# Banded attention unrolled into 19 rounds, with its bias table stored during the projection

## The reference, cut to what matters

```
s = einsum('bcqhgd,bckhd->bchgqk', qc, kb) * (HEAD_DIM ** -0.5)
bucket = t5_bucket(kpos[:, None, :] - qpos[:, :, None])
bias = rel_bias[bucket]
s = where(kmask, s + bias[None], -inf)
p = softmax(concatenate([s, sink], axis=-1), axis=-1)[..., :-1]
o = einsum('bchgqk,bckhd->bcqhgd', p, vb)
```

## Time and profile before

| | us |
|---|---|
| median of 3 runs | 2666.45 (2666.01 to 2674.58) |
| profiled execution | 2664.8 |
| its span | 2663.1 |
| TensorE busy in it | 2303.4 (86%) |
| DVE busy | 1716.6 (64%) |
| ACT busy | 1580.6 (59%) |
| POOL busy | 342.8 (13%) |

### The profile page before, as it was taken

The page is one execution under the profiler, slowest core; times in us unless marked ns, Lnnn a source line. Parts: engine busy times, 40 slices in busy tenths (PEclk is TensorE's granted clock), DMA queues, the critical chain, the costliest instruction groups (busy, mean ns, idle before and its releaser), DMA issues. The chain is left out here.

```text
span 2663.1 us, 36661 instructions
## 1 busy us (share of the span) xinstructions
PE 2303.4 (86%) x11322; PEld 1828.2 (69%) x11322; DVE 1716.6 (64%) x3034; ACT 1580.6 (59%) x2365; POOL 342.8 (13%) x425
## 2 busy tenths in 40 slices
PE   5999999917776999999997999279999999999980
PEld 4888888713444777777775888268888888888860
DVE  4314232135544787888774333579999999999986
ACT  5314342134543888877774433157888888788866
POOL 1101111100001000000000000021222222222221
PEclk9989999957886999999998999589999999999995
DMA  6425453151214222222004433279798878998847
GB/s 218 139 83 165 163 175 118 64 108 54 67 47 124 64 62 64 64 64 64 7 9 141 149 135 128 80 288 371 251 302 261 254 235 292 361 321 261 287 111 271
DMA packets 207042, 427.79 MB, mean 161 GB/s; under 512 B 37992, under 2 KB 84408, under 8 KB 205784
## 3 DMA queue, kind: packets, MB, share of 16 engines
q1 hardware_dynamic: 174872, 323.45, 35.6%
q0 software_dynamic: 32080, 103.20, 13.8%
HBM read 445.05 MB, written 86.39 MB: 200 GB/s over the span
## 5 line engine op out<-in xcount | busy, mean ns | idle before, releaser
L2285 DVE TENSOR_TENSOR moe_w_lo<-fetch_w_raw,moe_w_hi 128x1024 fp32r<-128x1024 f32 x376 | 434.9, 1216 | 8.5 <-ACT moe_w_hi L2214 8.3
L2214 ACT ACTIVATE moe_w_hi<-fetch_w_raw 128x1024 fp32r<-128x1024 f32 x376 | 368.3, 1053 | 67.5 <-PEq L90 36.3
L2339 PE MATMUL moe_ps_gu<-moe_w_hi,moe_xT_hi 128*128 128x512 f32 x736 | 293.1, 398 | 4.3 <-DVE moe_xT_lo L2296 4.3
L2341 PE MATMUL moe_ps_gu<-moe_w_hi,moe_xT_lo 128*128 128x512 f32 x736 | 289.0, 393 | 0.0
L2340 PE MATMUL moe_ps_gu<-moe_w_lo,moe_xT_hi 128*128 128x512 f32 x736 | 288.4, 392 | 0.0
L1260 ACT ACTIVATE fox_p<-fox_ps_t,fox_ncumT 128x512 f32<-128x512 f32 (+4 forms) x352 | 209.6, 595 | 117.7 <-PE fox_ps_t L1434 60.5
L461 PE MATMUL proj_ps_chunk<-proj_hT_hi,proj_w_hi 128*128 128x512 f32 (+1 forms) x576 | 234.6, 407 | 4.7 <-DVE proj_hT_lo L400 2.4
L1344 DVE TENSOR_TENSOR fox_p_lo<-fox_p,fox_p_hi 128x512 fp32r<-128x512 f32 (+4 forms) x352 | 199.2, 571 | 55.1 <-ACT fox_p_hi L1261 54.5
L463 PE MATMUL proj_ps_chunk<-proj_hT_hi,proj_w_lo 128*128 128x512 f32 (+1 forms) x576 | 231.4, 402 | 0.0
L462 PE MATMUL proj_ps_chunk<-proj_hT_lo,proj_w_hi 128*128 128x512 f32 (+1 forms) x576 | 230.9, 401 | 0.0
L1324 DVE CUSTOM_DVE_ANT_0 fox_ps_r<-fox_ps_r,fox_ncum 128x512 f32<-128x512 f32 (+4 forms) x352 | 198.0, 592 | 46.9 <-PE fox_ps_r L1404 25.9
(11 more groups left out here) (318 smaller groups left out, 5138.7 us busy)
## 6 DMA issues: line engine op xcount, KB each, us to landing
fetch_w_raw<-in_w_e_gate_dram SPq DMA_DIRECT2D x192, 512.0 KB
fetch_w_raw<-in_w_e_up_dram SPq DMA_DIRECT2D x192, 512.0 KB
fetch_d_raw<-in_w_e_down_dram SPq DMA_DIRECT2D x92, 1024.0 KB
proj_w_raw<-in_w_in_dram SPq DMA_DIRECT2D x24, 1536.0 KB, 8.0
proj_xt<-in_x_dram SPq DMA_DIRECT2D x16, 512.0 KB
h<-proj_hrow POOLq DMA_DIRECT2D x16, 512.0 KB, 3.2
qT<-proj_qk_out POOLq DMA_DIRECT2D x32, 256.0 KB, 3.3
win_q_raw<-qT SPq DMA_DIRECT2D x32, 256.0 KB, 3.8
```

Source lines behind the costliest of these rows:

```text
L2214: nc.scalar.activation(w_hi[:, k], w_raw[:, k].rearrange("p j n -> p (j n)"), ACT.Copy).then_inc(gu_high, 1)
L2285: nc.vector.tensor_tensor(w_lo[:, k], w_raw[:, k].rearrange("p j n -> p (j n)"), w_hi[:, k].bitcast(F32), ALU.subtract).then_inc(gu_split, 1)
L2339: nc.tensor.matmul(out, xT_hi[:, slot, k], w_hi[:, k, cols], start=k == 0, stop=False)
L2341: done = nc.tensor.matmul(out, xT_lo[:, slot, k], w_hi[:, k, cols], start=False, stop=k == KT - 1)
```

## The change

The bias table is now written and stored at the end of superblock 0 of the projection: SP loads `relT` near the projection's start, DVE makes the 31 copies behind the meta tokens' two, and POOL issues the store there. In the attention the three loads of the bias go out from POOL at once, without a wait for a store, and `bias0` is masked first; tile 0 needs only that one.

The hardware loop is gone. Every engine's list is 19 rounds written out. In round n TensorE and DVE make scores and biased scores of tile n, ACT the exponentials of tile n-1, TensorE, DVE and ACT turn and multiply tile n-2, and TensorE and DVE turn back and divide tile n-3. There are four buffers of raw queries and of values, three of split queries and of scores, two of `pT`; the score banks go from four to three, and the banks of turned probabilities from two to three. SP loads queries and values four tiles ahead. Keys are loaded in two pieces and split in four quads of four tiles, the first ahead of round 0, the others in rounds 0 to 2. The steps of the forget gates are spread over rounds 2 to 7. There is one `ntop` operation per tile in place of two, and the small memsets (`tick`, L824) are gone.

```diff
+        relT = m.sb("relT", [A_HEADS, N_BUCKETS])
+        table = m.sb("table", [A_HEADS, BIAS_TAB])
...
+                    pool.wait_ge(table_done, 1)
+                    pool.dma_start(t["table"][:, :, 0:BIAS_TAB],
+                                   table[:].unsqueeze(1).to_broadcast([A_HEADS, P, BIAS_TAB])).then_inc(table_stored, 16)
...
+                    dve.wait_ge(table_in, 16)
+                    for a, b, bucket in bucket_runs(-BIAS_R0, BIAS_TAB - 1 - BIAS_R0):
+                        done = nc.vector.tensor_copy(table[:, a + BIAS_R0:b + BIAS_R0 + 1],
+                                                     relT[:, bucket:bucket + 1].to_broadcast([A_HEADS, b - a + 1]))
+                    done.then_inc(table_done, 1)
...
-        q_raw = m.sb("q_raw", [P, 2, A_HEADS, P])
+        q_raw = m.sb("q_raw", [P, 4, A_HEADS, P])
...
-        s = m.sb("s", [P, 2, A_HEADS, SPAN])
+        s = m.sb("s", [P, 3, A_HEADS, SPAN])
...
-        pT = m.sb("pT", [P, 4, 4 * P])
+        pT = m.sb("pT", [P, 2, 4, 4 * P])
...
-        ps_s = [m.ps(f"ps_s{i}", [P, 2, 256]) for i in range(4)]
-        ps_pT = m.ps("ps_pT", [P, 2, 4 * P])
+        ps_s = [m.ps(f"ps_s{i}", [P, 2, 256]) for i in range(S_BANKS)]
+        ps_pT = [m.ps(f"ps_pT{i}", [P, 4 * P]) for i in range(T_BANKS)]
...
-        def tiles(engine, body):
-            body(0, 0, 0)
-            body(1, 1, 0)
-            body(2, 0, 1)
-            with engine.Fori(1, TILES // 2 - 1) as pair:
-                body(2 * pair + 1, 1, pair)
-                body(2 * pair + 2, 0, pair + 1)
-            body(TILES - 1, 1, TILES // 2 - 1)
...
+        LAST = TILES + 3
+        def rounds(body):
+            for n in range(LAST):
+                body(n)
...
-            sp.wait_ge(table_stored, 16)
...
+            def load_keys(piece, a, b):
+                for kv in range(A_KV):
+                    for half in range(2):
+                        sp.dma_start(k_raw[half * HD:half * HD + HD, kv, a:b],
+                                     t["kT"][kv * HD:kv * HD + HD, a - PAD:b - PAD]).then_inc(k_in[piece], 16)
...
+            load_keys(0, PAD, FIRST)
+            load_queries(0)
+            load_queries(1)
+            load_keys(1, FIRST, PAD + TOK)
+            load_queries(2)
+            load_queries(3)
+            for n in range(4):
+                load_values(n)
...
+            for n in range(4, TILES):
+                load_queries(n)
+                load_values(n)
...
+            for tensor, col, width, rel in ((bias, META, SPAN - META, META - PREV), (bias0, 0, META, -META),
+                                            (bias0, PREV, P, 0)):
+                pool.dma_start(tensor[:, :, col:col + width],
+                               bass.AP(tab.tensor, tab.offset + BIAS_R0 + rel,
+                                       [[BIAS_TAB, P], [P * (BIAS_TAB + 1), A_HEADS], [1, width]])).then_inc(bias_in, 16)
...
+            for n in range(TILES):
+                if n == 8:
+                    pool.wait_ge(dstep, 4)
+                    pool.dma_start(t["ncum"], fa[:]).then_inc(cum_stored, 16)
...
+            queries_high(0)
+            keys_high(0)
+            queries_high(1)
+            def body(n):
+                if n < TILES // QUAD - 1:
+                    keys_high(n + 1)
+                if n == 3:
+                    act.wait_ge(dstep, 1)
+                    nc.scalar.activation(fa[:], forget[:], ACT.Abs).then_inc(fstep, 1)
+                if n == 4:
+                    act.wait_ge(fstep, 1)
+                    nc.scalar.activation(fa[:], fa[:], ACT.Exp, scale=-1.0).then_inc(fstep, 1)
+                if n == 5:
+                    act.wait_ge(fstep, 2)
+                    nc.scalar.activation(fa[:], fa[:], ACT.Ln, bias=one[:]).then_inc(fstep, 1)
+                for half in range(2):
+                    if is_tile(n - 1):
+                        exponentials(n - 1, half)
+                    if is_tile(n - 2):
+                        copy_turned(n - 2, half)
+                if is_tile(n - 1):
+                    sink_exponentials(n - 1)
+                if is_tile(n + 2):
+                    queries_high(n + 2)
                 for kv in range(A_KV):
...
+                    if is_tile(n - 2):
+                        copy_outputs(n - 2, kv)
+            rounds(body)
...
+            def add_bias(n, pair):
+                add = bias0 if n == 0 else bias
+                if n <= 1 and pair == 0:
+                    dve.wait_ge(mask_ready, 2 * (n + 1))
+                    dve.wait_ge(bias_ready, 1)
+                if pair == 0:
+                    wait(dve, p_turned, 4 * (n - 2))
+                dve.wait_ge(s_done, 4 * n + pair + 1)
...
+            queries_low(0)
+            keys_low(0)
+            def body(n):
+                if is_tile(n):
+                    add_bias(n, 0)
+                    add_bias(n, 1)
+                if is_tile(n - 3):
+                    divide(n - 3, 0)
+                    divide(n - 3, 1)
+                if is_tile(n):
+                    add_bias(n, 2)
+                if is_tile(n - 2):
+                    copy_turned(n - 2, 0)
+                if is_tile(n):
+                    add_bias(n, 3)
+                    maxima(n)
+                if is_tile(n - 2):
+                    copy_turned(n - 2, 1)
+                if is_tile(n + 1):
+                    queries_low(n + 1)
+                if is_tile(n - 1):
+                    sums(n - 1)
+                if n < TILES // QUAD - 1:
+                    keys_low(n + 1)
+                if n == 2:
+                    nc.vector.tensor_scalar(forget[:], forget[:], b_forget[:], None, ALU.add).then_inc(dstep, 1)
+                if n == 3:
+                    dve.wait_ge(dstep, 1)
+                    dve.wait_ge(fstep, 1)
+                    nc.vector.tensor_scalar(forget[:], forget[:], 0.0, None, ALU.min).then_inc(dstep, 1)
+                if n == 6:
+                    dve.wait_ge(fstep, 3)
+                    dve.wait_ge(dstep, 2)
+                    nc.vector.tensor_tensor(forget[:], fa[:], forget[:], ALU.subtract).then_inc(dstep, 1)
+                if n == 7:
+                    dve.wait_ge(dstep, 3)
+                    nc.vector.tensor_tensor_scan(fa[:], one[:].to_broadcast([B_HEADS, TOK]), forget[:], 0.0,
+                                                 ALU.mult, ALU.add).then_inc(dstep, 1)
+            rounds(body)
...
+            def scores(n, pair):
+                if pair == 0:
+                    pe.wait_ge(q_split, n + 1)
+                    if n % QUAD == 0:
+                        pe.wait_ge(k_split, 4 * (n // QUAD + 1))
+                wait(pe, biased, 2 * (4 * n + pair - S_BANKS + 1))
...
+            def turn(n, i):
+                place = 4 * n + i
+                out = ps_pT[place % T_BANKS]
...
+            pe.wait_ge(zeroed, 2)
+            def body(n):
+                if is_tile(n):
+                    for pair in range(3):
+                        scores(n, pair)
+                if is_tile(n - 3):
+                    turn_back(n - 3, 0)
+                    turn_back(n - 3, 1)
+                if is_tile(n - 2):
+                    turn(n - 2, 0)
+                    turn(n - 2, 1)
+                if is_tile(n):
+                    scores(n, 3)
+                if is_tile(n - 2):
+                    turn(n - 2, 2)
+                    values(n - 2, 0)
+                    turn(n - 2, 3)
+                    values(n - 2, 1)
+            rounds(body)
```

384 lines of the change are left out of this document (135 added, 249 removed).

## The result

| | before | after |
|---|---|---|
| median, us | 2666.66 (4 runs) | 2602.42 (4 runs, 2599.49 to 2612.05) |
| ratio | 1 | 0.9759 [0.9735, 0.9782] |
| profiled execution / its span, us | 2664.8 / 2663.1 | 2612.05 / 2610.4 |
| load of `far` issued at (before, that of `relT` goes out just ahead of it, at 539.17) | 539.54 | 544.87 |
| first biased score at | 592.60 | 565.26 |

The change saves 64 us (58 to 71): faster, inside the range, 17 us short of the forecast of 2585. In the tables of this document the stage starts with the load of `far`, which both kernels have. Up to the next stage the two profiled executions differ by 65.4 us, and that is the difference that the terms have to make. Behind it the profiled execution after, the slowest of its four, is 12.7 us longer than that of before (1854.8 against 1842.1); I come back to it with the last experiment.

The account below looks back on a forecast made before the run. No engine is full; a latency sets the pace, DVE's first work on a tile waiting for ACT's last on the tile before. Start -39.6, tiles -48, projection +8: -80 us from 2664.8, so 2585 us; range 2562 to 2630.

Parts of the forecast that it names:

- Term 1: Attention's start: no wait for the table's store, POOL loads the bias at once, first biased score at 553: -39.6 us.
- Term 2: Steady rounds 3 to 15: TensorE's 8.15 us plus waits of 0.4 and 0.8, 9.4 us a round, 122 us.
- Term 3: Other tile time: rounds 0 to 2 25 us, gates 7, rounds 16 to 18 20; all tiles 174 against 222.2.
- Term 4: Projection: the table's store in POOL's queue holds up chunk 0's store and so ACT's chunk 3 copy: +8 us.
- my forecast with small errors: Whole kernel: the forecast holds but for small errors, 2572 to 2598 us; chance 50%.
- the clock rival: Attention rounds: TensorE's clock stays low over one product (2603 us) or both (2622); shares a 24% chance.
- the bias or projection at the bad end: Start or projection: either term at its unfavourable bound, 2598 to 2622 us; shares a 24% chance with low clock.
- The rival that the bias lands late: Start: bias on POOL's queue lands as late as the old store, leaving 22.6 of 39.6 us: 2602; within the 24%.
- the sign of being wrong that I had set at 560: Attention's start: the prediction is wrong if the bias comes later than 560 us on the old axis.
- the ring moves: Attention rounds: waits within a round add up to the old 13.64 us, 55 us lost, 2640; chance 10%.
- 7 us of them stick out: Forget gates in the rounds: DVE and ACT have some 1.5 and 2 us spare each, so 7 us lengthen the tiles.
- The weights that were to slow the table down: Projection: weight loads (1.5 MB) share the DMA engines and hold the table's store up; 8 us more would cost 11.

Follow-up runs that it names:

- experiment 12: The changed kernel run once more, unchanged, to check the stages behind the attention: 2607.43 us, ratio 0.977.
- experiment 11: Kernel before, unrolled, with DVE's low part of the next tile's queries moved behind the biased scores and copies: 2611.02 us, ratio 0.9787.
- (6): Kernel before with the attention's hardware loop written out and nothing else changed: 2665.09 us, ratio 0.9991.
- (8): Changed kernel with queries loaded only two tiles ahead rather than four, values still four ahead: 2605.39 us, ratio 0.9767.
- (7): Changed kernel with tile 0's queries loaded ahead of the first keys, and `bias0` loaded first and masked without waiting for the wide bias: 2603.31 us, ratio 0.9757.
- Experiment 4: Changed kernel with the last group of turned probabilities made ahead of the first product with the values on TensorE: 2586.96 us, ratio 0.969.
- (2): Changed kernel with the seven passes of the forget gates left out and their result set to zero: 2588.63 us, ratio 0.9699.
- Experiment 5: Changed kernel with the table's store issued on ACT's DMA queue in place of POOL's, at the same place of the projection: 2595.53 us, ratio 0.9727.

## Why the prediction was right, and where its sizes were off

Terms, each against its measured size (us; negative is saved):

| term | predicted | measured |
|---|---|---|
| 1, start | -39.6 | 53.1 to 20.4: -32.7 |
| 2 and 3, tiles | -48 | 222.2 to 183.9: -38.3 |
| 4, projection | +8 | 539.5 to 544.9: +5.3 |
| sum up to the next stage | -80 | -65.4 (0.3 lies behind the last division) |

**The total.** 2602.4 is inside the range, but outside the 50% that I gave to my forecast with small errors (2572 to 2598). It falls into the 24% for the clock rival or the bias or projection at the bad end, and close to the 2603 and 2602 that two rivals named. By the number alone one would believe them. The traces don't: undisturbed rounds are at a clock of 1.00 and the masks run at 556.20. What is missing lies in the gates and in the landing of the first queries.

**What bounds it.** The reading was right, and experiment 11 shows it more sharply than the changed kernel can. The pace was set by a latency, DVE's first work on a tile waiting for ACT's last on the one before, and moving that one step takes a tile from 13.67 to 9.89 us. The deeper pipeline takes another 0.2 us off a round, and nothing off the tiles' sum. The unrolling adds nothing that the medians show (6), and loading queries four tiles ahead rather than two nothing (8).

**Term 1: mechanism half right, size off by 7 us.** The masks came at 556.2 and the bias didn't set the start, as said. The keys' chain did, but it didn't "end nearly there": I had the first queries in by 547, from a row in which the keys had the engines to themselves, and allowed 4 us of sharing only to the bias. They were in 13.9 us behind the stage's start rather than 8, at a DMA share of 0.97 to 1.05; from there to the first biased score it took 6.4 us against the 6 forecast. So the landing of the queries is the term that was mis-sized. The sum for the masks was also loose: with three issues of 1.7 us each it gives 556, not 552, on the axis where they came at 551 (11.3 us behind the load of `far`). The rival that the bias lands late is refuted. That queries ahead of keys would help is refuted too (7); that fewer bytes in flight would help was not tried. The first biased score, 20.4 us behind the stage's start and not 14, comes at 559.9 on the old axis and just misses the sign of being wrong that I had set at 560.

**Term 2: right.** The forecast was 8.15 of TensorE and waits of 0.4 and 0.8; measured 0.37 and 0.78, a round of 9.69, and a clock of 1.00 in undisturbed rounds. Experiment 4 takes away exactly the two waits and leaves 8.55, so most of the 0.3 us between 9.4 and 9.69 lies in TensorE's own work: 8.55 less the wait of 0.16 that is left, 8.4, where I had 8.15 by counting starts. The rivals that the ring moves (13.64 per round) or that the clock stays low fall; before's low level did hang on its idle stretches, as experiment 11 shows.

**Term 3: the step that failed in size.** "7 us of them stick out" was 17.1 (2). I charged the gate passes by the slack of each engine over a round, 1.5 and 2 us. But three of the seven passes, Abs, Ln and the scan, delay a copy that TensorE waits for, and the slack ahead of that copy is not the round's: in round 5 Ln and two table loads, 4.6 us, become a wait of 3.68 in place of 0.78; then the clock falls, and the next products take 1.94 in place of 1.04. That round is 7.4 us longer than its neighbours (17.09 against 9.69), more than the pass itself; in experiments 5 and 7, where only the product right behind the same wait was slow, it takes 14.7. This is the clock rival in miniature, in 3 rounds (3, 5 and 8) rather than 13. Without the gates the tiles take 166.8, and the forecast without its 7 had 167; that near match is helped by small errors of both signs (13 rounds of 9.69 are 4 us more than 122, the other rounds 4 less).

**Term 4: right.** Chunk 3's copy waits for a DMA and comes at 233.94, 8.4 us behind the earlier trace rows against the 8 worked out; TensorE stands 3.15 us against 3.4 (6.0 in experiment 12), and the stage starts later. The start of the stage scatters: 536.3 to 539.6 in the six kernels without the table in POOL's queue (means 538.6), 542.3 to 545.6 in the eight with it (544.8). So the term is some 6 us. Experiment 5 shows the place in POOL's queue as its cause. The weights that were to slow the table down, for a cost of 11 us, did not show: it took 30.6 us from issue to landing against 29.5.

Of the 17 us between 2585 and 2602, 14.6 arise up to the next stage: the gates 10 and the start 7 too little saved, the projection 3 less spent. The rest is the difference between medians and one execution.

## What to carry to other kernels

When no engine is full, look for the first step of each engine's list on a new tile and what it waits for: one step that waits for another engine's last step closes a ring, and moving it may give all that a deeper pipeline gives (here tiles of 164.6 against 166.1 us). A long pass that is put "into the slack" of a pipelined round has to fit into the slack ahead of the next hand-over, not into that of the round; cut it into pieces or put it where its engine stands anyway. A store with few rows should not stand ahead of stores whose buffers somebody waits for in the same queue.

## What the runs showed of the hardware

- A wait of 3.7 us on TensorE was followed by products at the low level (1.94 us for two passes, 1.04 otherwise; in experiment 12, behind the same wait of 3.67 us, the first two passes still took 1.04 and the next 1.58 and 1.94) while waits of 0.4 to 0.8 us in every round left the granted clock at 1.00 (684 to 722 us). One wait of 1.95 us in round 3 was followed by a product of 1.04 and, behind a second wait of 0.78, by one of 1.94.
- An activation table load took 1.28 us and stood directly behind the operation before it (ended 612.87, load at 612.89, Ln at 614.18).
- Moving a store from POOL's to ACT's queue took 4.4 us off the wait of another store (9.44 to 5.03) but did not end it.
- In two executions of one program the stages behind the attention differed by 3.6 us, and the two tiles of before with both products at the low level, 6 us in all, did not come back in its unrolled twin.
